# Expert stage with sums fetched, added and stored block by block, rows finished at a token's second expert

## What is computed

```python
x = x + mix @ w_out                                   # the prefix: mLSTM heads and pooling
h = rmsnorm(x, norm2_g)
g = argmax(softmax(h @ w_rg + b_rg))                  # 1 of 4 groups
two experts of its 4 by h @ w_re + b_re, shares pv    # 16 experts in all
for e in chosen:                                      # w_gate, w_up: 1024 x 512, w_down: 512 x 1024
    x = x + gate[e] * ((silu(h @ w_gate[e]) * (h @ w_up[e])) @ w_down[e])
y = rmsnorm(x, norm_f_g)                              # y_prompt, y_sample
```

## Time and profile before

| | us |
|---|---|
| median of 3 runs (lowest, highest) | 935.23 (931.74, 937.87) |
| run of the profiled execution | 933.53 |
| its span, first to last instruction | 931.9 |
| TensorE busy | 876.2 (94%) |
| VectorE, POOL, ScalarE busy | 426.0, 374.8, 154.3 |
| moved by the DMA engines | 163.15 MB in 90039 packets |

### The profile page before, as it was taken

One profiled execution on the slowest core, in us unless ns is written; L12 is line 12 of the kernel. 1 busy time (PEld: TensorE's weight loads), 2 busy tenths in 40 slices (PEclk: granted clock), 3 DMA queues, 4 the chain that ended last, 5 costly groups with the idle time before them and its releaser, 6 DMA issues.

```text
span 931.9 us, 16630 instructions
## 1 busy us (share of the span) xinstructions
PE 876.2 (94%) x6339; PEld 751.6 (81%) x6339; DVE 426.0 (46%) x1106; ACT 154.3 (17%) x456; POOL 374.8 (40%) x575
## 2 busy tenths in 40 slices
PE   5989999999999999999999899999999999999950
PEld 3974987869688696885965899999999999999910
DVE  3244474644646446363468833333333333333264
ACT  2131212121211212111123210000000000000071
POOL 4040031210401204012150257777877777877514
PEclk9999999999999999999999999999999999999985
DMA  9840202130120300103019389999999999999883
GB/s 331 263 172 1 69 1 47 46 80 1 18 63 1 80 1 16 43 2 57 1 41 315 81 314 323 335 357 347 338 333 331 334 331 327 325 305 318 242 298 116
DMA packets 90039, 163.15 MB, mean 175 GB/s; under 512 B 48887, under 2 KB 59027, under 8 KB 81770
## 3 DMA queue, kind: packets, MB, share of 16 engines
q1 hardware_dynamic: 70062, 136.43, 42.0%
q0 software_dynamic: 17728, 25.28, 11.5%
q10 hardware_dynamic: 2188, 0.59, 0.3%
HBM read 139.83 MB, written 25.87 MB: 178 GB/s over the span
## 4 chain that ended last, share of the span: by engine, by line
PE 73%; issue 10%; DVE 7%; POOL 5%; DMA 3%; ACT 1%; POOLq 0%; SPq 0%; DVEq 0%; ACTq 0%
PE bank L1597 70%; POOL z_d L606 3%; PE bank L1602 2%; DMA wout<-h_d,idt 1%; DVE win L1552 1%; DMA mixT<-z_d 1%; POOL wout L558 1%; DVE wout L1513 0%; DVE wout L1483 0%; PE bank L1801 0%; PE bank L1714 0%; DMA xbuf<-in_x_prompt 0%; DMA z_d<-wout,win 0%; DVE wout L1506 0%; POOL out L726 0%
## 5 line engine op out<-in xcount | busy, mean ns | idle before, releaser
L1597 PE MATMUL bank<-wout,win 128*128 128x150 f32 (+3 forms) x2048 | 246.3, 282 | 1.2 <-DVE wout L1154 1.2
L1597 PEld LDWEIGHTS bank<-wout,win 128*128 128x128 f32 x2048 | 244.7, 190 | 1.2 <-DVE wout L1154 1.2
L1597 PE MATMUL bank<-hT,win 128*128 128x128 f32 (+1 forms) x1536 | 182.9, 279 | 0.0
L1597 PEld LDWEIGHTS bank<-hT,win 128*128 128x128 f32 x1536 | 178.6, 192 | 1.5 <-issue 1.2
L1597 PE MATMUL bank<-win 128*128 128x130 f32 (+5 forms) x1024 | 136.7, 293 | 1.3 <-DVE win L1498 1.1
L606 POOL DMA_INDIRECT z_d<-wout,win x75 | 125.4, 1672 | 27.1 <-issue 26.5
L1597 PEld LDWEIGHTS bank<-win 128*128 128x128 f32 (+2 forms) x1024 | 124.7, 190 | 11.2 <-issue 9.4
L1597 PE MATMUL bank<-win,hT 128*128 128x260 f32 (+3 forms) x512 | 121.0, 415 | 3.0 <-DVE xbuf L1287 1.5
L1597 PE MATMUL bank<-wout,mixT 128*128 128x512 f32 (+1 forms) x384 | 116.8, 487 | 1.8 <-ACT mixT L849 1.7
L1597 PEld LDWEIGHTS bank<-win,hT 128*128 128x128 f32 (+1 forms) x512 | 76.6, 172 | 42.3 <-issue 33.4
L1506 DVE STREAM_TRANSPOSE wout<-bank 128x480 f32<-128x480 f32 (+1 forms) x45 | 25.4, 605 | 160.3 <-DMA z_d<-wout,win 124.4
(11 more groups left out here) (316 smaller groups left out, 805.8 us busy)
## 6 DMA issues: line engine op xcount, KB each, us to landing
win<-in_w_gate SPq DMA_DIRECT2D x32, 1024.0 KB
win<-in_w_up SPq DMA_DIRECT2D x32, 1024.0 KB
win<-in_w_down SPq DMA_DIRECT2D x32, 1024.0 KB
win<-in_w_in SPq DMA_DIRECT2D x4, 2048.0 KB, 19.7
xbuf<-in_x_prompt SPq DMA_DIRECT2D x8, 512.0 KB, 3.7
wout<-in_w_out SPq DMA_DIRECT2D x1, 4096.0 KB, 15.1
z_d<-xbuf SPq DMA_DIRECT2D x32, 128.0 KB, 2.7
h_d<-xn SPq DMA_DIRECT2D x8, 512.0 KB, 2.7
```

Of the source, the lines that this page charges most:

```text
L1597: return nc.tensor.matmul(out, lhsT, rhs, start=first, stop=last)
```

## The change

- **List sizes.** Two lists of 150 first, then 5 x 128, 2 x 136, 2 x 140, 3 x 150, and two of 128 (`LR`) for the two smallest experts, which come last (`order`). With the counts above this is 150, 150, 5 x 128, 2 x 136, 2 x 140, 3 x 150, 128, 128, again 16 batches. The planner gets about ten more small steps for it. Where extra batches are needed, they go in ahead of the last two.
- **Down.** Every batch's down has the tokens stationary: `hid[:, k, 0:128]`, with 2 x 512 columns of `wd` moving, into banks 5 and 6. Slots past 128 are a second part, 8, 12 or 22 stationary columns: four products of 256 columns, one for each quarter, into partitions 0, 32, 64, 96 of bank 7.
- **Sums.** `z_d` now keeps natural order with four marks behind each quarter (rows of 1040). For each batch POOL fetches whole rows of the batch's tokens by index (`fetch_base`) into `Z`, VectorE adds share times the down result (`sums`) into `ZN`, and POOL stores plain rows back (`keep_sums`), no accumulating scatters, no transposes back. A mark says whether the token was seen: at its first expert a row's sum is stored to `z_d`, at its second the finished row goes to the output and not to `z_d` (indices of what isn't wanted are out of bounds).
- **Rows finished.** At the end of each batch ScalarE takes squares, Ln and Exp (`finish`) with two loads of its function table; VectorE in the next batch takes the root and scales (`rows_out`), POOL stores the rows (`store_rows`) one batch later. The tail with its nine tiles is gone.
- **Lists.** ScalarE loads each batch's tokens and shares (`load_tokens`) before its silus; VectorE makes the indices (`units_of`, `places_of`).
- **Prefix.** A tile's z is one store with pieces of 256 elements; ScalarE clears the marks with one transfer at tile 3; SP loads the norm weights behind the second expert's weights; VectorE waits for them at first use.
- `gather_scale` is in two parts and writes `xgT` in the order of the list (a step of five elements), so gate and up read N columns in a row.

The diff, cut to its core:

```diff
-    SLOTS = ((30, 1), (30, 1), (26, 6), (27, 2), (28, 2), (30, 2))
+    SLOTS = ((BLOCK, 1), (BLOCK, 1), (P, 5), (136, 2), (140, 2))
     NS = sum(n for _, n in SLOTS)
-    SIZES = [NP * r for r, n in SLOTS for _ in range(n)] + [BLOCK] * (NE - NS)
+    LR, FX = P, NE - 2
+    SIZES = [n for n, count in SLOTS for _ in range(count)] + [BLOCK] * (FX - NS) + [LR] * 2
+    SHORT = SIZES[:FX].count(P)
+    def longer_than(j0):
+        return sum(1 for n in SIZES[:j0 - 1] if n > P)
     NB = 2 * NE + 1
     assert NB >= NE + max((2 * TOK - m * min(SIZES)) // BLOCK + m for m in range(NE + 1))
...
-                for q in range(NQ):
-                    sp.dma_start(z_d[START[t]:START[t] + R, q * PIECE:(q + 1) * PIECE].rearrange("p (m i) -> p m i", m=KD),
-                                 xbuf[0:R, t % 4, :].rearrange("p (m q i) -> p m q i", m=KD, q=NQ)[:, :, q, :]
-                                 ).then_inc(S["x1_stored"], 16)
+                sp.dma_start(z_d[START[t]:START[t] + R, :].rearrange("p (q d) -> p q d", q=NQ)[:, :, 0:PIECE],
...
+            sp.dma_start(nfg, norm_f_g.rearrange("(a d) -> a d", a=1).broadcast_to([P, D])).then_inc(nf_in, 16)
+            sp.dma_start(nfq, norm_f_g.rearrange("(q d) -> q d", q=NQ).unsqueeze(1).broadcast_to([NQ, 32, PIECE])).then_inc(nf_in, 16)
...
+            def fetch_base(j):
+                pool.wait_ge(gi_ready, j)
+                stand(2)
+                g.indirect_dma_start(out=Z[:, 0:NQ, :].rearrange("p q d -> p (q d)"), out_offset=None, in_=z_d,
+                                     in_offset=bass.IndirectOffsetOnAxis(ap=gi[:, 0:1].bitcast(U32), axis=0)).then_inc(base_in, 16)
+                g.indirect_dma_start(out=Z[:, NQ, :], out_offset=None, in_=z_q,
+                                     in_offset=bass.IndirectOffsetOnAxis(ap=gi[:, 1:2].bitcast(U32), axis=0)).then_inc(base_in, 16)
+            def keep_sums(j, n):
+                pool.wait_ge(y_read, j + 1)
+                stand(3)
+                pool.wait_ge(idx_ready, j)
+                stand(6)
+                g.indirect_dma_start(out=z_d, out_offset=bass.IndirectOffsetOnAxis(ap=zi[:, 0:1].bitcast(U32), axis=0),
+                                     in_=ZN[:, 0:NQ, :].rearrange("p q d -> p (q d)"), in_offset=None,
+                                     bounds_check=TOK - 1, oob_is_err=False).then_inc(z_main, 16)
+                if n > P:
+                    g.indirect_dma_start(out=z_q, out_offset=bass.IndirectOffsetOnAxis(ap=zi[:, 1:2].bitcast(U32), axis=0),
+                                         in_=ZN[:, NQ, :], in_offset=None,
+                                         bounds_check=NQ * TOK - 1, oob_is_err=False).then_inc(z_over, 16)
+            def sums_kept(j, n, longer):
+                pool.wait_ge(z_main, 16 * j)
+                if n > P:
+                    pool.wait_ge(z_over, 16 * (longer + 1))
...
+            def store_rows(j, n, longer):
+                if not (isinstance(j, int) and j == 1):
+                    pool.wait_ge(out_over, 32 * longer)
+                    stand(7)
+                    pool.wait_ge(out_main, 32 * (j - 1))
+                stand(8)
+                g.tensor_copy(own, osi).then_inc(took, 1)
+                pool.wait_ge(took, j)
+                stand(0)
+                pool.wait_ge(out_ready, j)
+                stand(5)
+                send_rows(yt, own, n)
+            def send_rows(src, at, n):
+                for c, (dst, rows) in enumerate(((y_prompt[0], SEQ), (y_sample[0], DEC))):
+                    g.indirect_dma_start(out=dst, out_offset=bass.IndirectOffsetOnAxis(
+                        ap=at[:, 2 * c:2 * c + 1].bitcast(U32), axis=0), in_=src, in_offset=None,
+                        bounds_check=rows - 1, oob_is_err=False).then_inc(out_main, 16)
+                    if n > P:
+                        g.indirect_dma_start(out=dst.rearrange("t (q d) -> (t q) d", q=NQ), out_offset=bass.IndirectOffsetOnAxis(
+                            ap=at[:, 2 * c + 1:2 * c + 2].bitcast(U32), axis=0), in_=yo, in_offset=None,
+                            bounds_check=NQ * rows - 1, oob_is_err=False).then_inc(out_over, 16)
...
+            def turn(j, n, n_last, longer, more=True):
+                if more:
+                    load_ids(row_of(j + 3))
+                if n_last:
+                    store_rows(j - 1, n_last, longer - (n_last > P))
+                keep_sums(j, n)
+                if more:
+                    fetch_block(j + 3, range(3))
+                sums_kept(j, n, longer)
+                fetch_base(j + 1)
+                if more:
+                    gather_tokens([gathered] * NP, xg, range(3, NP))
...
+            def load_tokens(row):
+                act.dma_start(tokn[:, 0, :], ids_d[bass.ds(row, P), :]).then_inc(tok_in, 16)
+                act.dma_start(tokn[:, 1, :], ids_d[bass.ds(row + P, 32), :].unsqueeze(0).broadcast_to([NQ, 32, 2])).then_inc(tok_in, 16)
+            def finish(j, n):
+                act.preload_act_table_set("natural_log_exp_and_others")
+                act.wait_ge(y_read, j + 1)
+                last = a.activation(scrap[:, 0:D].rearrange("p (q d) -> p q d", q=NQ), body, ACT.Square, accum_out=fs[:, 0, 0:1])
+                if n > P:
+                    for q in range(NQ):
+                        last = a.activation(scrap4[0:32, q * PIECE:(q + 1) * PIECE], ZN[32 * q:32 * q + 32, NQ, 0:PIECE], ACT.Square,
+                                            accum_out=ss4[:, q:q + 1])
+                    last.then_inc(squared, 1)
+                    act.wait_ge(squared, 2 * j - 1)
+                    a.activation(scrap[0:32, D:D + NQ], ss4, ACT.Copy, accum_out=fs[0:32, 0, 1:2]).then_inc(squared, 1)
+                else:
+                    last.then_inc(squared, 2)
+                act.wait_ge(squared, 2 * j)
+                w = 2 if n > P else 1
+                a.activation(fs[:, 1, 0:w], fs[:, 0, 0:w], ACT.Ln, bias=epst[:, :], scale=1.0 / D).then_inc(logged, 1)
+                act.wait_ge(logged, j)
+                a.activation(fs[:, 2, 0:w], fs[:, 1, 0:w], ACT.Exp, scale=-0.5).then_inc(fs0, 1)
+                act.preload_act_table_set("silu_and_others")
+            def block_of(j, n, more=True):
+                if more:
+                    act.wait_ge(gi_ready, j)
+                    load_tokens(row_of(j + 1))
+                silus(j, n)
+                finish(j, n)
...
+            def units_of(j):
+                dve.wait_ge(tok_in, 32 * j)
+                chained(v.tensor_tensor(ub, tokn[:, :, 0], units[:, 0, :], ALU.mult), j, 1)
+                dve.wait_ge(y_read, j)
+                v.tensor_copy(tok, tokn)
+                v.tensor_tensor(ug, ub, units[:, 1, :], ALU.add)
+                v.tensor_tensor(gi, ub, units[:, 1, :], ALU.add).then_inc(gi_ready, 1)
+            def places_of(j, n):
+                v_past = past[:, RS.index(n - P) if n > P else 0, :]
+                dve.wait_ge(gi_ready, j)
+                opening = isinstance(j, int) and j == 1
+                chained(v.tensor_tensor(u, ug, v_past, ALU.add), j, 7, 6 if opening else 1)
+                v.tensor_scalar(ub, u, FAR, None, ALU.add)
+                chained(v.tensor_tensor(gap, u, units[:, 2, :], ALU.subtract), j, 8)
+                chained(v.tensor_scalar(out_of_range, gap, 0.0, FAR, ALU.is_lt, ALU.mult), j, 9)
+                chained(v.scalar_tensor_tensor(out=us, in0=gap, scalar=FAR, in1=out_of_range, op0=ALU.add, op1=ALU.add), j, STEPS)
+                dve.wait_ge(base_in, 32 * j)
+                if not opening:
+                    dve.wait_ge(took, j - 1)
+                v.scalar_tensor_tensor(out=zi, in0=seen, scalar=FAR, in1=u, op0=ALU.mult, op1=ALU.add)
+                v.scalar_tensor_tensor(out=osi[:, 0:2], in0=seen, scalar=-FAR, in1=ub, op0=ALU.mult, op1=ALU.add)
+                v.scalar_tensor_tensor(out=osi[:, 2:4], in0=seen, scalar=-FAR, in1=us, op0=ALU.mult, op1=ALU.add).then_inc(idx_ready, 1)
+                dve.wait_ge(idx_ready, j)
+                v.tensor_scalar(ZN[:, :, PIECE], Z[:, :, PIECE], 1.0, None, ALU.add)
+            def sums(j, n):
+                if n > P:
+                    dve.wait_ge(dn_done, 2 * j + 1)
+                    v.scalar_tensor_tensor(out=ZN[:, NQ, 0:PIECE], in0=B[YS][:, 0:PIECE], scalar=tok[:, 1, 1:2],
+                                           in1=Z[:, NQ, 0:PIECE], op0=ALU.mult, op1=ALU.add)
+                for c, b in enumerate(YB):
+                    dve.wait_ge(dn_done, 2 * j + c + 1)
+                    half = Z[:, 2 * c:2 * c + 2, 0:PIECE]
+                    last = v.scalar_tensor_tensor(out=ZN[:, 2 * c:2 * c + 2, 0:PIECE], in0=B[b][:, :].rearrange("p (q d) -> p q d", q=2), scalar=tok[:, 0, 1:2],
+                                                  in1=half, op0=ALU.mult, op1=ALU.add)
+                last.then_inc(y_read, 1)
+            def root_of(j, n, base, n0, by=1):
+                w = 2 if n > P else 1
+                dve.wait_ge(fs0, j)
```

(54 more changed lines are left out.)

505 lines of the change are left out of this document (191 added, 314 removed).

## The result

| | before | changed |
|---|---|---|
| median (lowest, highest), us | 935.28 (930.78, 937.87) | 950.16 (938.45, 970.36) |
| runs | 15 | 15 |
| ratio of the changed kernel to before, 95% interval | | 1.012 (1.0095 to 1.0146) |
| profiled execution's span, us | 931.9 | 948.9 |

Slower by 1.2%, where 915 us was forecast and slower had 0.08. The changed kernel's times also lie 32 us apart, those of before 7.

A forecast was written before the change was run, and what follows sets the result against it. The expert stage was taken to run at TensorE's pace. TensorE -3.4 us, tail -18.2 and loop with DMA engines +2 make -19.6: span 912.3, stated as 915 us on the median, range 905 to 929.

The forecast's parts named there:

- start of the first down: First batch's down: the planner ends later but still before 541.71 us, so the start stays there; prefix 0.
- gate and up, batches 2 to 16, waits left out: TensorE in the expert stage: 4 x 16.32 + 7 x 14.3 + 2 x 14.9 + 2 x 15.3 = 225.8 us.
- down, 16: TensorE's down with tokens stationary: 16 x 0.436 = 7.0 us a batch whatever its size, 111.5 us for 16 batches.
- overs, 9: Products for slots past 128 in nine long batches: 1.8 us each, 16.7 us, four running side by side.
- waits of TensorE: Waits in the expert stage from the serial loop and the DMA engines together: +2 us.
- tail: Behind the last matmul: 14.6 us in place of 32.8, -18.2 us; 6.6 of it after the last store's issue.
- POOL and the serial loop: POOL's stores, landings, fetches and places between batches: loop of 18.7, 23.0 or 27.2 us; with DMA engines +2 us.
- rival 2: Narrow products of the overs don't run side by side at 8 to 22 columns: +46 us, 961; chance 0.07.
- rival 1: Serial loop or DMA engines set the pace of batches 3 to 7: +10 to +26 us, 924 to 940; chance 0.16.
- Rivals 3 and 4: 3: last rows land behind one another, 7 us more, 922; 4: VectorE's steps fit worse, 929; chance 0.05 each.
- the doubled end of the range: VectorE's scale of the gathered rows: 1.48 us, or 3.0 if writes at a step of five elements double it.
- granted clock under 1.00: Named sign of being wrong: TensorE's granted clock falls under 1.00 in the expert stage.

The follow-up runs named there:

- control: The changed kernel, unedited, run again beside its own variants: 919.1 us on chip 2, 950.8 on chip 6, 977.9 on chip 3, 919.5 on chip 5.
- row cut: In long lists' turns POOL fetches bases first, waits for the next gate and up's end, then gathers; against the control: 927.7 us (chip 3), 928.1 (chip 5).

## Why the prediction was wrong

**The sum itself held.** In the control's profile without stalls the span is 916.4 (chip 2) where the sum gave 912.3. Term by term, from that timeline:

| term | forecast | measured | difference |
|---|---|---|---|
| start of the first down | 541.7 | 539.9 | -1.8 |
| gate and up, batches 2 to 16, waits left out | 225.8 | 226.3 | +0.5 |
| down, 16 | 111.5 | 109.9 | -1.6 |
| overs, 9 | 16.7 | 20.4 | +3.7 |
| waits of TensorE | 2 | 3.7 | +1.7 |
| tail | 14.6 | 16.2 | +1.6 |
| span | 912.3 | 916.4 | +4.1 |

The total is nearer than its terms: 7.5 us over and 3.4 under cancel in part, which is luck. The first term came out lower because the first gate and up began at 523.36 and not at 525.29; the sum had priced the prefix at nothing, and why it got shorter was not looked for.

On chips 2, 6, 3 and 5 the ratio to before was 0.981, 1.013, 1.046 and 0.980; the forecast's was 0.978.

**The step that failed** stands under "POOL and the serial loop". It took "a long turn is about 21 us of POOL's time against 25.1" as relief, and priced POOL's issues only by POOL's own time and by what waits for their data. That POOL's turn can slow TensorE while nothing waits for it was priced at nothing, and none of the rivals held it: each rival had a wait with a name, and the stall has none. In place of nothing the runs showed 33.3 us of stalls in the profile after, 27.6 and 54.5 on chips 6 and 3, and none on 2 and 5. Nor did a row of before show it: there POOL was busier (374.8 us against 335.0), and in a batch of 130 it issued five scatters of 1.55 us and five gathers of 0.95 in a row of 11 with the list, with no stall of TensorE. But most of its scatters stand beside the down before, and its last issue is out at 623.8, 6.5 us into the gate and up that starts at 617.28. The new row has 14 in the long batches, of which the later ones fall in the second half of gate and up, where the stalls are. Whether it is this place or the kind of transfer was not tried.

**Overs.** 2.26 to 2.28 us each and not 1.8: 32 instructions at 71 ns, where the row of the prefix gave 29 ns for half the columns. They do run side by side at 8, 12 and 22 columns (rival 2 is out), but at twice the columns an instruction cost 2.4 times as much, not twice. The Trainium skill (TensorE: Matmul & The Clock Gate, Part 3) has 2.38x for three column tiles, which the prediction weighed as 2.9 us more for the nine and set aside; the runs have 3.7 more, so the page was nearer than my row.

**The tail.** 16.2 us. The last scale ends at 904.53, the last issue at 907.59, and the span at 916.4 (chip 2):

```profile
900.29 0.75 DVE L1563 SCALAR_TENSOR_TENSOR xbuf<-bank,mixT,wout 128x512 f32<-128x512 f32 x1 [0.96 <-PE bank L1644]
...
901.14 1.06 ACT L941 ACTIVATE hT<-xbuf 128x1024 f32<-128x1024 f32 x1 [6.14 <-DVE xbuf L1563]
...
903.78 0.75 DVE L1639 TENSOR_SCALAR xbuf<-xbuf,fs 128x1024 f32<-128x1024 f32 x1
...
905.34 0.98 POOL L657 DMA_INDIRECT out<-xbuf,mixT  x1 [0.54 <-issue]
906.63 0.96 POOL L657 DMA_INDIRECT out<-xbuf,mixT  x1 [0.30 <-issue]
```

The engines' part came out as forecast: from the last matmul at 900.25 to the last issue's end 7.3 us, against 8.0. What was taken too short is the end behind the last issue, 8.8 us for the 6.6 of before, whose last issue was an indirect store of rows as well; why this one lands later was not tried.

**Loop and DMA engines** (rival 1): not bound where it was feared. Short batches ran 21.2 to 22.0 us apart, at 365 to 385 GB/s and shares of 1.01 and 1.02 in 600 to 680 us of the changed kernel's profile, over the 351 that I had as a lower bound, and TensorE waited 0.6 and 0.5 us, ahead of the downs of batches 3 and 5. The reserve is small: a second load of each list cost 11.7 us. Rivals 3 and 4 did not come either: the tail was 1.6 us over and the waits 1.7, where they had 7 and 14.

**VectorE.** The scale into steps of five elements took 2 x 1308 ns for 1.48 us, near the doubled end of the range. In the unedited kernel it showed in one place only, ahead of batch 2, where TensorE waits up to 1.2 us for it.

**Clock.** The granted clock under 1.00, which the prediction named as a sign of being wrong, was there: it follows the stalls. From 740 to 750 us, in the stall of batch 10, TensorE is busy 0.8 to 1.7 us of every 2; the granted clock is 0.80 in 748 to 750, 0.50 in 750 to 752, the 1.2 GHz level, and 0.84 in 752 to 754.

**What stays open.** The cause of the stalls stays open: which resource POOL's issues or their transfers and TensorE's instructions share, why the controls of chips 2 and 5 show no stall, that of 6 some and that of 3 the most, whether room between issues would help, and what the new row has that the row of 11 before had not. The trace shows TensorE without a wait, its signals up to 8 us late and SP slow between two issues, so I suspect the path of instructions and signals rather than SBUF or the DMA engines, whose share falls to 0.26 to 0.52 in 738 to 746 us; that is an argument from these rows, not shown, and part of the low share is only that SP's next weights were issued late. The Trainium skill (DMA: Bandwidth & Descriptors, SWDGE vs HWDGE vs iDMA) says that descriptors of POOL's transfers are written to rings in SBUF, and names an interference of VectorE with that; no run here shows it to be this one.

No version that computes all of the layer was best everywhere. The changed one was best where it had no stalls (0.98) and worse than before elsewhere (1.01 to 1.05); the one with the row cut was at 0.99 on one chip of either kind (3 and 5), so it is the safer choice of the two. Leaving out the sample stores points to the better one, a turn of POOL with fewer issues, if `y_sample` can be had in another way.

## What to carry to other kernels

When an edit gives POOL more transfers, price them also by where their issue falls: count the issues in a row, and see which products of TensorE run beside them; here it was mostly the short products with a new stationary operand each that suffered. A stall in which the waits name only "issue" and a signal comes late is a thing of its own: look for the engine whose row of work ends with it, and run the unedited kernel beside every variant and on more than one chip before a cause is named. Each term of the sum on paper came within 4 us of its measured value; what missed was a term that no row of before had.

## What the runs showed of the hardware

- TensorE's instructions can be held up with no wait that the profile knows: in batch 10 of the profile after, 64 instructions took 15.8 us in place of 7.7, and SP's issue that waits for the last one before them came 8.2 us after its record. What POOL issues beside them bears on it: 54.5 us of such stalls with the row in one piece and 9.6 with it cut (chip 3), 27.6 with the sample stores and 0.5 without (chip 6).
- It differs by chip or occasion: 54.5, 27.6, 0 and 0 us of such stalls for the same program on chips 3, 6, 2 and 5, while the median of the kernel before varied by 0.3% over them.
- Products in four groups of 32 output partitions cost 71 ns an instruction with 256 moving columns (8 to 22 stationary ones), and 29 ns with 128 (32 stationary ones).
- From the end of the last indirect store's issue to the end of the span it took 8.8 us (chip 2), and 6.6 in the kernel before.
- A multiplication of 1280 float32 columns on VectorE took 1.48 us with its results in a row, and 2 x 1.31 us in two parts that write with a step of five elements.
